# Attention steps in another order: turn of the probabilities, scores, then the product with the values

## The chip, the cores and the metric

One core of a Trainium2 chip runs one program. The time is device microseconds (us) of an execution. The kernel before took 1731.72 us, the median of three runs (1726.76 to 1733.15). Five engines work side by side, each with its own queue of instructions in order: TensorE (PE in the rows; PEld is its loading of weights), VectorE (DVE), ScalarE (ACT), GpSimd (POOL) and SyncE (SP). They meet through semaphores only.

## The reference

Two layers of a hybrid trunk run over 384 tokens (256 latent, 128 context), width 1024, in float32. Each layer has four token mixers on the same normalised input (A: mLSTM; B: neighbourhood attention with a bias table, 8 heads; C: sliding-window attention with a sink, 8 query heads on 2 key heads; D: differential attention, 4 heads of two maps), a gated merge of their outputs, an output projection, and a mixture of experts. The part that the change touches is

```python
s = q @ k.T * scale (+ bias or window, + sink logit)
p = softmax(s)                 # D: p = softmax(s0) - lam * softmax(s1)
out = p @ v
```

Latent queries see the 256 latent keys and 128 cached ones; context queries see the 128 context keys.

## The kernel before

**The list of steps.** The function `schedule()` writes the whole layer out as one list, `SCHEDULE`, and every engine's program walks this list and issues its own part of each step (`for s in SCHEDULE`). So a step's place in the list is its place in the queues of TensorE, VectorE and ScalarE alike. Both layers run the same loop body.

**Gemm units.** The backbone of the list is 102 units `("gemm", g)`. A unit is 128x1024 weights in float32, which ScalarE splits into a high part `whi` (L974) and GpSimd into a low part `wlo` (L810), two units ahead; TensorE takes three products per block (L1340 to L1342), 18 matmuls for three token tiles, into the banks `G`. `("rest", g, t)` is the remainder of a unit from tile t on, so that steps can stand inside a unit. In `branch` units VectorE evicts `G` (L1999), in `proj` and `gate` units ScalarE does.

**Attention.** A unit of attention is a type (B, C, D), a token tile t (0, 1 latent; 2 context, with 128 keys only) and j of 4: 12 units per type, two heads or two maps each. `attention(g, first)` lays their steps out as a pipeline of 15 slots, i = 0 to 14, one after each gemm unit from g on for i < 9, and two per unit after that. A slot holds `sn` of unit i-1, `pv` of i-3, `pt` of i-2 and `sc` of i. What each step issues:

- `sc`: TensorE computes the scores into the banks `S0` and `S1` (L1638, L1639, or L1641 for the context tile). VectorE adds the bias or window (L1860, `prob<-S,bias`, types B and C of latent tiles), takes the maximum (L2144) and its negative (L2151; C has three small instructions). ScalarE takes the exponentials (L1183; C also one of the sink), and issues the load of the next bias, and after the last unit of a type the load of keys.
- `sn`: VectorE takes the reciprocal (L2160) and scales `prob` (L2168; D: L2162 to L2164).
- `pt`: TensorE transposes `prob` into the banks `T0` and `T1` (L1652); ScalarE copies `T0` (L1200) and, in B and C, VectorE copies `T1` (L2175) into `probT`.
- `pv`: TensorE multiplies by the values into the bank `O` (L1682, B and C, 64 output rows at a time; L1679, D). In B and C ScalarE copies `O` rounded to `bhi` (L1212) and VectorE then subtracts it from `O` into `blo` (L1860, `blo<-O,bhi`); in D ScalarE alone copies it (L1206). After the last unit of a type ScalarE issues the load of the next values.

`prob`, `probT` and the softmax's small tiles have two buffers, used in turn by unit; `S`, `T` and `O` have one set. Before TensorE writes a bank, `free(...)` makes it wait for the engine that last read it: `pv` waits for the `blo` (D: the copy) of the unit before, `pt` for the copies of `T0` and `T1`.

**What else shares these queues and banks.** `mod` (L1397): in every fourth such step TensorE multiplies four weight blocks into `O`; it waits until `O` is free. `modv` copies the result on ScalarE (L1134), `modt` turns it in `T1` (L1420). `tp` (L1558) turns `q` and `k` of the next type in the `T` banks, with copies by ScalarE (L1145, L1148). `rope`: VectorE rotates `q` and `k` of D, three tensor_tensor and then two (L1860, `pB<-pA,rope_t` and `pA<-pB`), placed behind the slots that follow gemm 43, 45, 47 and 49 (type B's slots 3, 5, 7 and, two slots later in the list, 10). B's attention starts at gemm 40, C's at 52, D's at 64; `mod` steps stand after the first tile of gemm 55, 59, 67, 71, 76 and others.

The order within a slot comes from the order of the `append` calls in `attention` alone.

Of the kernel before, what the change touches and what calls it, by code (L numbers as in the profile page):

```python
# [108 lines left out]
def schedule():  # L109

    after = {g: [] for g in range(-1, NG)}
    inner = {}

    def put(g, *steps):
        after[g] += steps

    def put_inside(g, t, *steps):

        inner.setdefault((g, t), []).extend(steps)

    put(0, *(("mod", j) for j in range(NEXT, NEXT + MQ)))
    put(1, ("quad3",))
    put(0, ("dma", "stateC"))
    put(4, ("mgate",))
    put_inside(5, 1, ("mturn",))
    put(5, ("tp", "A", "q", 0), ("tp", "A", "q", 1))
    put(6, ("tp", "A", "q", 2), ("tp", "A", "q", 3), ("mcum",))
    put(9, ("tp", "A", "k", 0), ("tp", "A", "k", 1))
    put(10, ("tp", "A", "k", 2), ("tp", "A", "k", 3))
    for m in range(len(MU)):  # L130
        put(9 + 4 * m, ("md", m))
        put(11 + 4 * m, ("m1", m))
        put(13 + 4 * m, ("m2", m))
        put(14 + 4 * m, ("m3", m))
    put(LAST_UNIT[CHUNK_NO["Bv"]] + 2, ("dma", "outB"))
    put(LAST_UNIT[CHUNK_NO["Ckv"]] + 2, ("dma", "outC"))
    put(35, ("dma", "loadB"), ("hn", 0))
    put(37, ("hr", 0))
    for i in range(4):
        put(36 + i, ("tp", "B", "q", i), ("tp", "B", "k", i))  # L140
    put(LAST_UNIT[CHUNK_NO["Dv"]] + 2, ("dma", "outD"))

    def attention(g, first):
        for i in range(12 + 3):
            at = []
            if 1 <= i < 13:
                at.append(("sn", first + i - 1))
            if i >= 3:
                at.append(("pv", first + i - 3))
            if 2 <= i < 14:  # L150
                at.append(("pt", first + i - 2))
            if i < 12:
                at.append(("sc", first + i))
            if i < 9:
                put(g + i, *at)
            elif i % 2:
                put_inside(g + 9 + (i - 9) // 2, 1, *at)
            else:
                put(g + 9 + (i - 9) // 2, *at)
        return g + 12  # L160

    g = attention(40, 0)
    for i in range(4):
        put(40 + i // 2, ("to", 0, i))
    for at, r in zip(ROPE_AFTER, ROPE):
        put(at, ("rope",) + r)
    for i in range(4):
        put_inside(g - 3 + i // 2, 2, ("tp", "C", "q", i))
    put_inside(g - 1, 2, ("tp", "C", "k", 0), ("tp", "C", "k", 1))
    g = attention(g, 12)  # L170
    for i in range(4):
        put_inside(g - 3 + i // 2, 2, ("tp", "D", "q", i))
        put_inside(g - 1 + i // 2, 2, ("tp", "D", "k", i))
    g = attention(g, 24)
    put(g, ("hn", 1))
    put(g + 1, ("hr", 1))
    for i in range(4):
        put(g + 5, ("to", 1, i))
    d_done = g + 5
    for j in range(16, NMOD):  # L180
        q = 36 + j // MQ * MQ + MQ - 1
        q += q in (63, 75)
        put_inside(q, 1, ("mod", j))
        if j % KD == KD - 1:
            put_inside(q, 1, ("modv", j // KD))
            put(37 + j, ("modt", j // KD))
    put(36 + 30, ("gt", 0))
    put(36 + 33, ("gout", 0))
    put(36 + 50, ("gt", 1))
    put(36 + 53, ("gout", 1))  # L190
    put(g - 5, ("dma", "gate1"))
    for c in range(4):
        put(FIRST_UNIT[CHUNK_NO["branch", (3, 1)]], ("mt", c))
    for c in range(4, 8):
        put(FIRST_UNIT[CHUNK_NO["wout", 0]] + 1, ("mt", c))
    put(max(d_done, LAST_UNIT[CHUNK_NO["gate", (3, 0)]]), ("dma", "loadX"))

    steps = [("norm", 0), ("prepare",)]

    for g in range(NG):  # L200
        steps.append(("gemm", g))
        if g == 1:
            steps.append(("dma", "saveX"))
        for t in range(1, TILES):
            if (g, t) in inner:
                steps += inner[g, t] + [("rest", g, t)]
        steps += after[g]
    branch3 = steps.index(("gemm", FIRST_UNIT[CHUNK_NO["branch", (3, 0)]]))
    assert d_done < NG
    late = [s for s in steps[branch3:] if s in [("to", 1, i) for i in range(4)] or s in (("hn", 1), ("hr", 1)) or  # L210
            (s[0] in ("sc", "sn", "pt", "pv") and s[1] >= 24)]
    steps = steps[:branch3] + late + [s for s in steps[branch3:] if s not in late]
    steps += [("norm", 1)] + [("mod", j) for j in OFFRING] + [("route",), ("experts",), ("end",)]
    return steps
# [2226 lines left out]
```

How the kernel before makes its waits and increments, by code:

```python
        @block.sync  # L647
# [13 lines left out]
                def need(s, i):  # L661
                    sp.wait_ge(s.handle, s.value(l, i))
# [3 lines left out]
                def released(p):  # L666
                    if p < 0:
                        sp.wait_ge(*e_lo.in_tile(l, 0, UT, p))
                    elif gs[p] is None:
                        sp.wait_ge(*mod_pe.at(l, ORDER[p][1] - NEXT))
                    else:
                        sp.wait_ge(*lo_done.at(l, gs[p]))
# [2 lines left out]
                    w_in[p % RAW].of(sp.dma_start(raw[:, p % RAW, :], a["units"][bass.ds(l * NU + p, 1), :, :]  # L677
                                                  .rearrange("a p n -> p (a n)")))
                def layer_of(name, n=1):
                    return a[name][bass.ds(l, 1)]
                pc_in.of(sp.dma_start(pcol[:, :], layer_of("pcol").rearrange("a p n -> p (a n)")))
                for p in range(RAW):
                    released(p - RAW)
                    load(p)
                sp.wait_ge(*layer_end.at(l, -1))
                for i in range(MQ):
                    lq_in.of(sp.dma_start(late_home[i], a["units"][bass.ds(l * NU + (RINGN + NEXT + i), 1), :, :]
                                          .rearrange("a p n -> p (a n)")))
# [8 lines left out]
                        p += 1  # L699
                    elif s == ("dma", "saveX"):
                        sp.wait_ge(tokens_in, 16 * TILES)
                        sp.wait_ge(*layer_end.at(l, -1))
# [91 lines left out]
                def need(s, i):  # L794
                    pool.wait_ge(s.handle, s.value(l, i))
```

## Time and profile before

| what | value |
|---|---|
| median of three runs | 1731.72 us (1726.76 to 1733.15) |
| the profiled execution | 1727.18 us, of which the span of the trace is 1725.2 us |
| granted clock of TensorE, mean | 0.997 |
| busy: TensorE, VectorE, ScalarE, GpSimd | 97%, 61%, 51%, 38% |
| type B's attention, layer 0 | about 249 to 329 us from the span's start |
| type C's | about 333 to 413 us |
| type D's | from about 420 us |

A row of a timeline has the start in us from the span's start, the duration in us, the engine, the line, the operation, output<-inputs, the shape (for matmuls rows*columns of the array in use, then the moving operand) and a count; in brackets stands idle time of the engine just before it and what ended it. Instructions of one group that follow each other are merged in one row. Matmuls overlap, so the distance from start to start is what one costs. `whi` rows on ScalarE stand in the gemm step that follows a slot.

### The profile page before, as it was taken

The page shows a single profiled execution, that of the slowest core. Times are in us where ns is not written, and L with a number is a line of the kernel's source. Part 1 is how long each engine was busy: PE and PEld are TensorE (multiplying, and loading weights), DVE is VectorE, ACT ScalarE, POOL GpSimd, SP SyncE. Part 2 cuts the span into 40 slices and gives each one's busy share as a digit, 9 for nine tenths or more (in the row PEclk, how much of TensorE's full clock was granted, in tenths as well). Part 3 has the DMA queues.
Part 4 walks back from the last instruction along what each step waited for, and adds up shares of the span by engine and source line. Part 5 has one row for each costly group of instructions (what it writes and reads, how often), then busy time and mean ns, then how long its engine had stood idle before and what let it go on. Part 6 is the DMA issues. An engine that isn't in the chain of part 4 may idle for free.

```text
span 1725.2 us, 30932 instructions
## 1 busy us (share of the span) xinstructions
PE 1667.7 (97%) x9997; PEld 1329.3 (77%) x9997; DVE 1045.9 (61%) x1868; ACT 872.9 (51%) x1499; POOL 661.8 (38%) x426
## 2 busy tenths in 40 slices
PE   6999999999999999999989999999999999999997
PEld 5788787677888877777767888777778887777775
DVE  3127577564461189999850374775635413899997
ACT  2443344444443357788644334454445334587874
POOL 0645563334467621011125555533344765201102
PEclk9999999999999999999999999999999999999999
DMA  8723343343555559999865234334354553999994
GB/s 335 269 90 103 105 147 125 102 178 136 186 196 217 184 192 408 372 370 366 304 224 196 98 104 138 108 121 146 123 184 160 208 200 142 336 385 370 372 365 157
DMA packets 120847, 367.46 MB, mean 213 GB/s; under 512 B 11964, under 2 KB 34044, under 8 KB 120704
## 3 DMA queue, kind: packets, MB, share of 16 engines
q1 hardware_dynamic: 95024, 323.99, 51.9%
q0 software_dynamic: 6624, 24.18, 3.6%
q10 hardware_dynamic: 19056, 17.52, 3.3%
q8 instruction: 73, 1.20, 0.3%
q14 instruction: 70, 0.57, 0.1%
HBM read 341.71 MB, written 23.93 MB: 212 GB/s over the span
## 4 chain that ended last, share of the span: by engine, by line
PE 52%; issue 17%; DVE 14%; POOL 8%; ACT 4%; DMA 3%; SPq 1%; ACTq 0%; DVEq 0%; POOLq 0%
PE G L1340 13%; PE G L1342 12%; PE G L1341 11%; POOL wlo L810 6%; DVE wlo L1860 4%; ACT whi L982 2%; PE O L1397 2%; PE T L1652 2%; PE S L1638 1%; DMA x_scratch<-pA 1%; DVE pA L1860 1%; PE O L1682 1%; PE S L1340 1%; DVE pB L1860 1%; PE S L1342 1%
## 5 line engine op out<-in xcount | busy, mean ns | idle before, releaser
L810 POOL TENSOR_TENSOR wlo<-raw,whi 128x1024 fp32r<-128x1024 f32 x198 | 483.0, 2445 | 571.3 <-ACT whi L974 571.2
L1340 PE MATMUL G<-whi,hhi 128*128 128x512 f32 (+1 forms) x1440 | 578.5, 402 | 12.3 <-DVE wlo L1860 6.4
L1342 PE MATMUL G<-whi,hlo 128*128 128x512 f32 (+1 forms) x1440 | 557.7, 387 | 0.0
L1341 PE MATMUL G<-wlo,hhi 128*128 128x512 f32 (+1 forms) x1440 | 557.1, 387 | 0.0
L1340 PEld LDWEIGHTS G<-whi,hhi 128*128 128x128 f32 x1440 | 270.4, 188 | 90.7 <-DVE wlo L1860 16.5
L1342 PEld LDWEIGHTS G<-whi,hlo 128*128 128x128 f32 x1440 | 270.5, 188 | 57.5
L1341 PEld LDWEIGHTS G<-wlo,hhi 128*128 128x128 f32 x1440 | 271.1, 188 | 46.9
L974 ACT ACTIVATE whi<-raw 128x1024 fp32r<-128x1024 f32 x204 | 214.6, 1054 | 106.9 <-PE G L1342 71.2
L1860 DVE TENSOR_TENSOR wlo<-raw,whi 128x1024 fp32r<-128x1024 f32 x150 | 179.8, 1220 | 6.3 <-ACT whi L982 3.3
L982 ACT ACTIVATE whi<-raw 128x1024 fp32r<-128x1024 f32 x144 | 152.6, 1060 | 32.5 <-PE G L1342 18.5
L1183 ACT ACTIVATE prob<-prob,am 128x384 f32<-128x384 f32 x64 | 38.9, 609 | 117.0 <-DVE am L2151 58.7
L982 ACT ACTIVATE whi<-pA 128x1024 fp32r<-128x1024 f32 x72 | 76.4, 1062 | 41.7 <-PE G L1342 23.0
L1860 DVE TENSOR_TENSOR wlo<-pA,whi 128x1024 fp32r<-128x1024 f32 x72 | 88.0, 1224 | 15.5 <-ACT whi L982 13.3
L1860 DVE TENSOR_TENSOR wlo<-pB,whi 128x1024 fp32r<-128x1024 f32 x72 | 85.2, 1224 | 6.9 <-ACT whi L982 6.3
L1340 PE MATMUL S<-whi,ehi 128*128 128x512 f32 x192 | 79.4, 414 | 6.4 <-DVE elo L1860 6.3
L982 ACT ACTIVATE whi<-pB 128x1024 fp32r<-128x1024 f32 x72 | 75.1, 1057 | 10.9 <-PE G L1342 10.6
L1340 PE MATMUL G<-whi,bhi 128*128 128x512 f32 x192 | 79.2, 412 | 0.0
L1342 PE MATMUL S<-whi,elo 128*128 128x512 f32 x192 | 75.4, 393 | 0.0
L1341 PE MATMUL S<-wlo,ehi 128*128 128x512 f32 x192 | 75.2, 391 | 0.0
L1342 PE MATMUL G<-whi,blo 128*128 128x512 f32 x192 | 75.1, 391 | 0.0
L1341 PE MATMUL G<-wlo,bhi 128*128 128x512 f32 x192 | 74.9, 390 | 0.0
L805 POOL TENSOR_TENSOR sink_col<-ones 128x1 f32<-128x1 f32 x26 | 15.5, 597 | 149.7 <-ACT yo L1276 76.8
(384 smaller groups left out, 2411.0 us busy)
## 6 DMA issues: line engine op xcount, KB each, us to landing
raw<-in_units SPq DMA_DIRECT2D x426, 512.0 KB, 5.1
pA<-in_units SPq DMA_DIRECT2D x78, 512.0 KB, 5.9
pB<-in_units SPq DMA_DIRECT2D x72, 512.0 KB, 6.3
h_sorted<-sig POOLq DMA_DIRECT2D x12, 514.0 KB, 7.1
hs<-h_sorted POOLq DMA_DIRECT2D x10, 514.0 KB, 7.4
y_sorted<-yo POOLq DMA_DIRECT2D x10, 512.0 KB, 7.1
bias<-in_nat_bias ACTq DMA_DIRECT2D x16, 256.0 KB, 3.2
kT<-in_units SPq DMA_DIRECT2D x6, 512.0 KB, 4.8
```

What stands on the lines that cost most here:

```text
L810: lo_done.of(nc.gpsimd.tensor_tensor(wlo[:, k, :], raw[:, POS_OF[g] % RAW, :], whi[:, k, :].bitcast(F32), ALU.subtract))
L974: hi_done.of(nc.scalar.activation(whi[:, g % CONV, :], raw[:, p % RAW, :], ACT.Copy))
L982: hi_done.of(nc.scalar.activation(whi[:, n % CONV, :], expert_raw(n), ACT.Copy))
L1183: e = nc.scalar.activation(prob[:, u % 2, m, 0:w], src, ACT.Exp, bias=am[:, u % 2, m:m + 1], accum_out=am[:, u % 2, 2 + m:3 + m])
L1340: nc.tensor.matmul(dst, st_hi, mv_hi, start=start, stop=False)
L1341: nc.tensor.matmul(dst, st_hi, mv_lo, start=False, stop=False)
L1342: return nc.tensor.matmul(dst, st_lo, mv_hi, start=False, stop=stop)
L1397: mm = nc.tensor.matmul(O[32 * q:32 * q + 32, c0:c0 + P], cond[:, k, :], raw[:, MODPOS[j - MQ + 1 + q] % RAW, k * P:(k + 1) * P], start=(k ...
L1638: nc.tensor.matmul(S[:, m, 0:256], q, kT[r, kj, 0:256], start=True, stop=True)
L1652: mm = nc.tensor.transpose(T[:, m, b * P:(b + 1) * P], prob[:, u % 2, m, b * P:(b + 1) * P], ident[:, :])
L1682: mm = nc.tensor.matmul(O[64 * m:64 * m + 64, 0:P], values(b, lo, 64), pr, **fl)
L1860: return V.tensor_tensor(o, i0, i1, op)
```

## The change

In `attention`, the `append` of `pv` moves behind those of `pt` and `sc`. A slot is then `sn` of unit i-1, `pt` of i-2, `sc` of i, `pv` of i-3, on every engine that has a part in them. Slots with two of the steps (12, 13) turn `pv`, `pt` into `pt`, `pv`; slots 0 to 2 and 14 are as before. Each step's instructions, waits and buffers are unchanged.

```diff
@@ -145,12 +145,12 @@
             at = []
             if 1 <= i < 13:
                 at.append(("sn", first + i - 1))
-            if i >= 3:
-                at.append(("pv", first + i - 3))
             if 2 <= i < 14:
                 at.append(("pt", first + i - 2))
             if i < 12:
                 at.append(("sc", first + i))
+            if i >= 3:
+                at.append(("pv", first + i - 3))
             if i < 9:
                 put(g + i, *at)
             elif i % 2:
```

## Rows read from the trace of the kernel before

**Rows 1.** The profile page, busy time (share of the span) and instructions of each engine.

```profile
PE 1667.7 (97%) x9997; PEld 1329.3 (77%) x9997; DVE 1045.9 (61%) x1868; ACT 872.9 (51%) x1499; POOL 661.8 (38%) x426
```

**Rows 2.** Timeline of TensorE, slot 3 of type B, and slot 5's start (start us, duration us, engine, line, what, count).

```profile
267.54 0.39 PE L1342 MATMUL G<-whi,hlo 128*128 128x512 f32 x1
...
267.86 0.66 PE L1682 MATMUL O<-probT,pB 128*64 128x128 f32 x8
...
268.66 0.88 PE L1652 MATMUL T<-ident,prob 128*128 128x128 f32 x6
...
269.47 0.71 PE L1638 MATMUL S<-kT,qT 64*128 64x256 f32 x4
...
270.33 0.50 PE L1340 MATMUL G<-whi,hhi 128*128 128x512 f32 x1
...
281.42 0.66 PE L1682 MATMUL O<-probT,pB 128*64 128x128 f32 x8
```

**Rows 3.** Timeline of TensorE: slot 2 of type C; slot 14 of type B.

```profile
343.42 0.39 PE L1342 MATMUL G<-whi,hlo 128*128 128x512 f32 x1
...
343.66 0.81 PE L1652 MATMUL T<-ident,prob 128*128 128x128 f32 x6
...
344.40 0.71 PE L1638 MATMUL S<-kT,qT 64*128 64x256 f32 x4
...
328.69 0.44 PE L1682 MATMUL O<-probT,pB 128*64 128x128 f32 x4
...
329.06 0.50 PE L1340 MATMUL G<-whi,hhi 128*128 128x512 f32 x1
```

**Rows 4.** Timelines of VectorE, ScalarE and GpSimd, type B, slots 3 to 7.

```profile
270.80 0.96 DVE L1860 TENSOR_TENSOR prob<-S,bias 128x768 f32<-128x768 f32 x1 [0.24 <-DMA bias<-in_nat_bias]
...
273.06 1.36 DVE L1860 TENSOR_TENSOR pB<-pA,rope_t 128x512 f32<-128x512 f32 x3
...
275.33 2.90 DVE L2168 TENSOR_SCALAR prob<-prob,am 128x384 f32<-128x384 f32 x2
...
278.15 0.28 DVE L1860 TENSOR_TENSOR blo<-O,bhi 128x128 fp32r<-128x128 f32 x1
...
278.35 0.54 DVE L2175 COPY probT<-T 128x384 f32<-128x384 f32 x1
...
278.81 0.94 DVE L1860 TENSOR_TENSOR prob<-S,bias 128x768 f32<-128x768 f32 x1
...
297.16 0.75 DVE L2168 TENSOR_SCALAR prob<-prob,am 128x384 f32<-128x384 f32 x2
...
274.20 1.04 ACT L974 ACTIVATE whi<-raw 128x1024 fp32r<-128x1024 f32 x1
...
289.89 0.26 ACT L1212 ACTIVATE bhi<-O 128x128 fp32r<-128x128 f32 x1
...
275.32 2.36 POOL L810 TENSOR_TENSOR wlo<-raw,whi 128x1024 fp32r<-128x1024 f32 x1 [3.24 <-ACT whi L974]
```

**Rows 5.** Timelines of VectorE and GpSimd, a rope step of the mLSTM stretch.

```profile
147.89 2.40 DVE L1860 TENSOR_TENSOR pB<-pC,rope_t 128x512 f32<-128x512 f32 x1
...
147.34 5.21 POOL L810 TENSOR_TENSOR wlo<-raw,whi 128x1024 fp32r<-128x1024 f32 x2 [6.02 <-ACT whi L974]
```

**Rows 6.** Timeline of TensorE, two waits in attention: slot 9 of B, slot 12 of C.

```profile
307.21 0.66 PE L1682 MATMUL O<-probT,pB 128*64 128x128 f32 x8 [1.76 <-DVE probT L2175]
...
406.92 0.44 PE L1652 MATMUL T<-ident,prob 128*128 128x128 f32 x2 [0.99 <-ACT qT L1145]
```

**Rows 7.** Timelines of TensorE and ScalarE around `mod`, in type C and in type D.

```profile
376.13 1.95 PE L1397 MATMUL O<-raw,cond 128*32 128x128 f32 x64
...
379.53 1.04 ACT L974 ACTIVATE whi<-raw 128x1024 fp32r<-128x1024 f32 x1
...
460.46 1.96 PE L1397 MATMUL O<-raw,cond 128*32 128x128 f32 x64
...
461.41 1.05 ACT L974 ACTIVATE whi<-raw 128x1024 fp32r<-128x1024 f32 x1
```

## The prediction

> **What bounds the kernel now.** I read first the busy times: TensorE is busy for 97% of the span [rows 1], so whatever lengthens or shortens TensorE's own queue in the attention stretch appears in the time one for one, and whatever happens on other engines counts only where TensorE waits for it. Then TensorE's timeline through one attention slot: between two gemm units come the product with the values (`pv`), the turn of the probabilities (`pt`), and the scores (`sc`) [rows 2]. Then VectorE, ScalarE and GpSimd through the same slots, because the list of steps is walked by every engine: the diff moves the eviction of `O` behind the softmax of the newer unit on ScalarE and VectorE too. I write E for the moment when ScalarE has finished a slot's exponentials and starts its next instruction. In the before kernel VectorE spends the time up to E on other work, the rope step above all: its row starts 1.14 us before E, while the exponentials run [rows 4]. The second layer's attention rows repeat the first's, so all that follows is worked out for layer 0 and doubled.
>
> **What is removed: one switch of the array's shape per slot, on the path.** For the unit types B and C, `pv` is 128*64, `sc` is 64*128, and gemm and `pt` are 128*128. From the last gemm matmul to the next one, a full slot takes 0.32 + 0.80 + 0.81 + 0.86 = 2.79 us [rows 2]. With `pt` first, gemm to `pt` is 0.24 and `pt` to `sc` 0.74, seen in a slot that has no `pv` [rows 3]. `pv` to gemm costs what `pv` to `pt` does: 0.37 for four matmuls [rows 3], 0.80 for twelve [rows 2]. Only `sc` to `pv` is shown nowhere. A switch shows as 0.08 us ahead of it (0.32 against 0.24) and 0.07 behind it (0.81 against 0.74), 0.15 in all. From below `sc` to `pv` costs no switch (0.15 less than `sc` to gemm), from above two (0.15 more); I take 0.86 as for `sc` to gemm, the nearest row, since it too is one switch. The new slot is 0.24 + 0.74 + 0.86 + 0.80 = 2.64, a gain of 0.15 us (0 to 0.3). Nine slots of B and nine of C per layer have all three steps: 18 x 0.15 = -2.7 us per layer. Type D's `pv` is 128*128, and keeps its number of switches: 0. The Trainium skill, page TensorEngine Tiling (Array Packing), section Key Properties, says that changing the tiling mode drains TensorE. That speaks for the change; by the whole 0.39 us of a gemm matmul per drain it would be -7 us per layer instead; rows 2 and 3 show less than half of that.
>
> **What is added: the eviction of `O` stands behind the exponentials.** The copy `bhi` (0.26 us) now runs at E, and VectorE's `blo` waits for it, at E + 0.3. Behind `blo` in VectorE's queue stand the rope step, the branch evictions, the next normalisation (`sn`), the copy of `T1`, and the next scores' bias add. Who waits: the next `pv` and the `mod` matmuls (both want `O`), and `pt` (wants `sn` and `T1`).
> A plain slot: `blo` at E + 0.3, reciprocal E + 0.5, scaling E + 0.7 (0.75 us [rows 4]), copy of `T1` E + 1.4, bias add E + 1.85. From bias add to its own E it is 274.20 - 270.80 = 3.4 us [rows 4], so the next E is at E + 5.25.
> A slot with rope (four of B's): rope starts at E + 0.5 instead of before E. GpSimd's `wlo` subtraction began 1.12 us after E and lasted 2.36 [rows 4]; with the copy ahead of `whi` it runs from about E + 1.3 to E + 3.7. VectorE is held by such an instruction: the 2.90 us of two scalings that take 0.75 elsewhere [rows 4], and one rope instruction of 2.40 us where three take 1.36 [rows 5]. Two of the rope instructions (0.45 each) get through before it, the rest (2.27 - 0.9 = 1.4 up to the scaling) follows: scaling at E + 5.1, copy at E + 5.8, bias add at E + 6.25, next E at E + 9.65.
> The Trainium skill, page SBUF — State Buffer, section Who interferes with whom, gives this as a rule: two-input VectorE instructions and GpSimd exclude each other. By this rule, the trace agrees, and the rope cannot slip through.
> VectorE's pair of slots becomes 14.9 us. TensorE's is 281.42 - 267.86 = 13.56 us [rows 2], less 0.3 for two switches. VectorE, hidden until now, is 1.6 us too slow per pair.
> - Slot 5: `pv` wants `O` at 281.42 - 0.38 + 1.60 = 282.64; it is free at 274.20 + 9.65 + 0.6 = 284.45: +1.8 us.
> - Slot 7: the same excess again, +1.6 us.
> - Slot 9: `pt` waits for the copy of `T1` and `sc` for the exponentials, together 3.5 us, less the 1.76 us that stand there now [rows 6]: +1.7 us.
> - Slots 10 and 12: `pt` now has nothing in front of it while the copies of the turned `q` and `k` leave the `T` banks; the turn between them waits for a later `T1` copy: +0.45, +0.6, +0.5. The same wait in type C is 0.99 us now, behind `pv` [rows 6]; there it costs +0.65 and +0.3.
> Sum of B: 6.7 - 1.3 = +5.4 us per layer.
> **C.** No rope, so VectorE keeps up (5.5 us against 6.6), with the branch evictions too. But after slot 6 four `mod` matmul groups want `O` at 376.13 - 0.6 = 375.5, and slot 6's E is 379.53 [rows 7], 1.15 us earlier in the new order because `sc` no longer stands behind `pv` and three slots are shorter. `O` is free at E + 0.6 = 379.0: +3.5 us. The next turn of `mod` values no longer waits 0.2 us. C: 3.5 + 0.95 - 0.2 - 1.35 = +2.9 us.
> **D.** VectorE has no part in its `pv`. The `mod` matmuls at 460.46 want `O`, whose copy ends 0.28 us after E, 461.41 - 0.67 [rows 7], so at 461.0: +0.6 us. The scores' 0.67 us earlier start is otherwise covered by gemms.
> Queues: no DMA moves past another; the bias loads keep their place in the `sc` step, the loads of keys and values theirs, SP's and GpSimd's lists are unchanged. The split into `whi` comes 0.16 us later per slot and up to 2 us later behind a late E; its result is wanted a whole gemm unit (some 4 us) later, so it costs nothing; without that cover it would be those 2 us again.
>
> **Sum.** 5.4 + 2.9 + 0.6 = 8.9 us per layer, +17.9 us in all. Against the profiled execution (1727.2 us) this gives 1745.1; the median of the runs shown lies 4.5 us higher, so 1749.6 by it, and one of its three runs is as low as the profiled one. I forecast 1748.
>
> **Rivals.**
> *Rope escapes the hold* (it starts early enough, or GpSimd later). Then only the scaling is held, until E + 3.7 as now; VectorE's pair is 13.5 us, B costs about +0.9 instead of +5.4: 4.4 x 2 = +9 us, 1740. For it: the margin at the third rope instruction is 0.1 us. Against it: the instructions behind the third would be caught instead [rows 5].
> *C's scaling is caught as well.* In C one small instruction more stands ahead of it, so its second half starts about E + 1.25, GpSimd at E + 1.3. If GpSimd wins, each C slot's `sn` is 2.3 us later, VectorE needs 8.4 us per slot against 6.6, and the wait at `mod` grows by about 4 us per layer: 1757.
> *The other side: the saved switches decide.* If `O` is never late (the copy at E + 0.3 is reached before `pv` asks, because the earlier `sc` pulls E forward by more than rope pushes it back), only -2.7 us per layer is left: 1726, within 0.5%. It decides once E + 0.6 lies before `pv`'s turn, 1.6 us after the slot begins; in plain slots this holds with over 1 us in hand, in the slots after rope it misses by 1.8. The drain rule of the Trainium skill named above, at its full 0.39 us per switch, would make this one 1717.
> *The order of the other engines doesn't matter* (the change acts as its words say, on TensorE alone): then -5 us from switches and the three stalls kept, the same 1726. The code speaks against it, since all engines walk one list.
>
> **How the numbers follow.** Forecast 0.48; rope escapes 0.14; C caught too 0.16; saved switches, by either way, 0.22. About 0.5% (8.6 us) is what a measurement of this kernel can tell from no change. Slower by more than that: 0.48 + 0.16 + half of the rope case (1740 lies on the bound) = 0.71. The 0.22 splits into 0.06 faster, if a switch costs more than I take, and 0.16 the same, with the other half of the rope case 0.23. The range goes from 1728, between the switch case and the rope case, to 1760, past the C case. The forecast's own range is 1742 to 1754.
>
> **What would show it.** Right: in the waits of TensorE, new rows in which `O` (the lines of `pv` and of `mod`) waits for `blo` by VectorE, 1.5 us each in slots 5 and 7 and 3.5 us at C's `mod`; rope rows on VectorE of 3 us or more beside a `wlo` row of GpSimd; full slots of 2.64 us instead of 2.79. Wrong: rope still at 1.36 us, no wait at `mod`, or full slots as long as before. If no wait on `O` is over 1 us, my account of VectorE's queue fails as a whole; if the waits are there and the slots of B lag by less than 1 us each, only the hold by GpSimd does.

## The result, and the profile after

The changed kernel takes 1765.21 us (median of four runs, 1761.8 to 1766.3) beside 1729.24 for the kernel before on the same chip: 1.0206 times as long, 95% interval 1.019 to 1.0221. I had forecast 1748, with a range from 1728 to 1760. The sign was right, and the size was half of what came: +17.9 us forecast, +36 measured.

The page's busy times of the changed kernel:

```profile
PE 1681.4 (95%) x9997; PEld 1343.4 (76%) x9997; DVE 1047.0 (59%) x1868; ACT 869.8 (49%) x1499; POOL 659.8 (37%) x426
```

TensorE has the same 9997 matmuls as in [rows 1], but is busy for 13.7 us more. The switches that were saved should not have made this more. So besides new waits, some matmuls ran slower. The span of the trace rose by 39.4 us, of which 25.7 are idle time of TensorE.

The waits of TensorE, whole span (the bank it wanted, its line, who let go of it: us in total, times, longest):

```profile
PE O L1682 <- DVE blo L1860: 9.5, 6, 1.7
PE O L1397 <- issue: 6.9, 2, 3.5
...
PE T L1652 <- DVE probT L2175: 5.5, 2, 2.8
...
PE O L1397 <- ACT pA L1206: 3.8, 2, 1.9
PE T L1558 <- DVE probT L2175: 3.6, 2, 1.8
PE T L1652 <- ACT qT L1145: 2.6, 4, 0.9
PE T L1652 <- DVE modc L1860: 2.3, 2, 1.2
```

The forecast's new waits are all here: `pv` (L1682) on `blo`, and `mod` (L1397) on the bank `O`. Two more are not in my sum: the last row, and a third wait per layer in the first row (I had two, slots 5 and 7). Every count is a multiple of two, one for each layer.

TensorE's timeline, type B, layer 0: slot 3 whole, then the rows with a wait in slots 5, 7 and 9 and in the turn of C's `q`:

```profile
270.03 0.39 PE L1342 MATMUL G<-whi,hlo 128*128 128x512 f32 x1
270.26 0.82 PE L1652 MATMUL T<-ident,prob 128*128 128x128 f32 x6
271.00 0.71 PE L1638 MATMUL S<-kT,qT 64*128 64x256 f32 x4
...
271.87 0.66 PE L1682 MATMUL O<-probT,pB 128*64 128x128 f32 x8
...
272.67 0.50 PE L1340 MATMUL G<-whi,hhi 128*128 128x512 f32 x1
...
286.77 0.66 PE L1682 MATMUL O<-probT,pB 128*64 128x128 f32 x8 [1.56 <-DVE blo L1860]
...
301.78 0.66 PE L1682 MATMUL O<-probT,pB 128*64 128x128 f32 x8 [1.66 <-DVE blo L1860]
...
313.26 0.88 PE L1652 MATMUL T<-ident,prob 128*128 128x128 f32 x6 [2.79 <-DVE probT L2175]
314.64 0.49 PE L1641 MATMUL S<-kT,qT 64*128 64x128 f32 x4 [0.50 <-ACT prob L1183]
315.13 1.12 PE L1682 MATMUL O<-probT,pB 128*64 128x128 f32 x8
...
328.87 0.55 PE L1558 MATMUL T<-ident,pC 128*128 128x128 f32 x3 [1.76 <-DVE probT L2175]
```

The slot is 272.67 - 270.03 = 2.64 us, as worked out, against 2.79 in [rows 2]. The waits in slots 5, 7 and 9 (1.56, 1.66 and 2.79 + 0.50) are near the prediction's 1.8, 1.6 and 3.5. The row at 315.13 is the surprise: eight matmuls that take 0.66 us everywhere else take 1.12.

TensorE's timeline again: C's and D's `mod` matmuls, and in C the `pv` of slot 6 and the turn of slot 9:

```profile
384.04 0.66 PE L1682 MATMUL O<-probT,pC 128*64 128x128 f32 x8 [1.67 <-DVE blo L1860]
...
389.97 3.55 PE L1397 MATMUL O<-raw,cond 128*32 128x128 f32 x64 [3.47 <-issue]
...
407.94 0.84 PE L1652 MATMUL T<-ident,prob 128*128 128x128 f32 x6 [1.15 <-DVE modc L1860]
...
478.63 3.48 PE L1397 MATMUL O<-raw,cond 128*32 128x128 f32 x64 [1.88 <-ACT pA L1206]
```

The same stretches in the table of windows (busy time of each engine, then the granted clock):

```profile
core 0: us, PE busy (x) PEld busy (x) DVE busy (x) ACT busy (x) POOL busy (x), PEclk, DMA share, GB/s
...
315.00:318.40 3.40, 3.40 (x20) 2.64 (x17) 2.25 (x11) 2.32 (x8) 0.00 (x0) 0.50 0.02 5
390.00:393.50 3.50, 3.50 (x65) 3.12 (x65) 0.88 (x3) 0.49 (x1) 2.56 (x1) 0.52 0.02 5
478.80:482.30 3.50, 3.50 (x65) 3.12 (x58) 1.01 (x3) 0.73 (x1) 2.45 (x1) 0.51 0.02 5
```

Three times per layer TensorE comes back from a long wait and is granted the lower of its two levels, 1.2 GHz instead of 2.4, for some 3.4 us. `mod` then takes 3.55 and 3.48 us instead of the 1.95 and 1.96 of [rows 7]. The trace of before shows no such fall in attention, not even behind its wait of 1.76 us [rows 6].

Laid side by side, the two traces part by 35.4 us in attention: 6.7 in B, 7.0 in C and 4.3 in D in layer 0, and 17.5 in all in layer 1. The other 4 us lie at the first gemm units (2.3, from 31 to 54 us) and between the layers (1.6). The change touches nothing there. The clock does: the changed kernel's trace has a granted clock of 0.72 from 30 to 36 us and of 0.59 from 892 to 896, and the trace of before has 1.00 at both places. Such falls come and go there in the traces of the other kernels below too, so I don't count these 4 us to the change.

### The profile page after: what moved, and what is told of

Read it like the earlier page. It is cut to its first block, busy times and chain, and to the rows that moved or that the text cites. A ratio compares the mean times of both kernels' runs of the same rounds, so it can differ in the third digit from the quotient of the medians.

```text
span 1764.6 us, 30952 instructions
## 1 busy us (share of the span) xinstructions
PE 1681.4 (95%) x9997; PEld 1343.4 (76%) x9997; DVE 1047.0 (59%) x1868; ACT 869.8 (49%) x1499; POOL 659.8 (37%) x426
## 3 DMA queue, kind: packets, MB, share of 16 engines
q8 instruction: 75, 1.23, 0.3%
## 4 chain that ended last, share of the span: by engine, by line
PE 52%; DVE 18%; issue 14%; POOL 5%; ACT 5%; DMA 4%; SPq 1%; ACTq 1%; DVEq 0%; POOLq 0%
PE G L1340 13%; PE G L1342 12%; PE G L1341 12%; DVE wlo L1860 4%; POOL wlo L810 4%; ACT whi L982 2%; PE O L1397 2%; DVE pB L1860 2%; DVE am L2144 2%; DMA x_scratch<-pA 1%; DVE pA L1860 1%; PE S L1340 1%; DVE prob L1860 1%; DMA bias<-in_nat_bias 1%; ACT prob L1183 1%
## 5 line engine op out<-in xcount | busy, mean ns | idle before, releaser
L1183 ACT ACTIVATE prob<-S,am 128x128 f32<-128x128 f32 (+1 forms) x80 | 35.5, 449 | 81.4 <-DVE am L2151 67.7
```

The source lines that it names most:

```text
L1183: e = nc.scalar.activation(prob[:, u % 2, m, 0:w], src, ACT.Exp, bias=am[:, u % 2, m:m + 1], accum_out=am[:, u % 2, 2 + m:3 + m])
```

## The experiments

In all of them `schedule` takes a function that gives `pv`'s place in a slot: 0 first as before, 1 behind `pt`, 2 last as in the changed kernel. TensorE, ScalarE and VectorE may each walk a list of their own:

```diff
-            if i >= 3:
-                at.append(("pv", first + i - 3))
+            pv = [("pv", first + i - 3)] if i >= 3 else []
+            place = where(first, i)
+            if place == 0:
+                at += pv
             if 2 <= i < 14:
                 at.append(("pt", first + i - 2))
+            if place == 1:
+                at += pv
             if i < 12:
                 at.append(("sc", first + i))
+            if place == 2:
+                at += pv
...
-                for s in SCHEDULE:
+                for s in WALK["pe"]:
```

The diffs below show only these places. Line numbers in these kernels are 10 higher (`rope ahead` 14; with dummies 11 to 17). Every ratio is against the kernel before on the same chip.

**Which engine's order costs?** First TensorE's order alone:

```diff
+PE_WHERE = lambda first, i: 2
+ACT_WHERE = lambda first, i: 0
+DVE_WHERE = lambda first, i: 0
```

> TensorE walks the new order (turn, scores, values); ScalarE and VectorE keep the old one (eviction of O first). Theory 1 (the loss comes from the eviction's place on ScalarE and VectorE, not from TensorE's order): the waits for O at slots 5 and 7 of type B and at the mod steps are gone, no half-clock window in attention, full slots stay 0.15 us shorter; 1729 - 5 + 2 for the turns that wait for the T banks = 1726 (1720 to 1732). Rival (TensorE's own order costs it): at least 1755.

Measured: 1745.11 us, 1.0088 (1.0072 to 1.0105). Both missed. No wait on `O` over 0.3 us is left, but VectorE now stands at `blo` for a `pv` that comes late, ahead of its copy of `T1` (in slot 3 for 0.96 us, 0.16 in the kernel before). TensorE's wait for that copy rose to 3.1 us in slot 9, and the clock fell behind it. In C four waits of 0.95 to 1.60 us on the `T` banks and the scores cost about 3 us more per layer. Then the other two engines' order alone:

```diff
+PE_WHERE = lambda first, i: 0
+ACT_WHERE = lambda first, i: 2
+DVE_WHERE = lambda first, i: 2
```

> The opposite split: TensorE keeps the old order, ScalarE and VectorE take the new one (eviction of O behind the exponentials). Theory 1: as slow as the changed kernel or slower, since O is free as late and TensorE asks for it 1.6 us earlier in a slot: 1770 (1760 to 1785), with the waits for O on the line of the values in slots 5 and 7. Rival (TensorE's order costs it): 1729.

Measured: 1779.39 us, 1.028 (1.0263 to 1.0297), as the theory said, and the worst of all. Its waits of TensorE:

```profile
PE O L1692 <- DVE blo L1870: 29.9, 21, 3.7
...
PE O L1407 <- issue: 6.2, 2, 3.1
```

`pv` asks for `O` at the head of the slot and gets it behind the exponentials. So most of the loss comes from the place of the eviction, and a late `pv` on TensorE softens it; but TensorE's new order alone isn't free either.

**The eviction ahead of the exponentials, TensorE still in the new order.**

```diff
+PE_WHERE = lambda first, i: 2
+ACT_WHERE = lambda first, i: 1
+DVE_WHERE = lambda first, i: 2
```

> TensorE in the new order; ScalarE copies O ahead of the exponentials (turn, values, scores); VectorE subtracts behind the new maximum (turn, scores, values), while the exponentials run. Theory 1: what hurts is the copy behind the exponentials, which makes VectorE wait for them; here VectorE's part is covered, rope stays at 1.4 us, no wait for O over 0.5 us: 1725 (1719 to 1731). Rival (anything of the eviction behind the scores on VectorE costs): over 1740.

Measured: 1733.88 us, 1.0023 (1.0014 to 1.0033). Of the 36 us all but 4 are gone. The only difference from the changed kernel is the place of one 0.26 us copy per unit on ScalarE. The miss of 9 us against my 1725 has one place; TensorE's timeline at C's `mod`:

```profile
379.60 3.46 PE L1407 MATMUL O<-raw,cond 128*32 128x128 f32 x64 [2.44 <-issue]
```

`blo` still stands behind VectorE's part of the scores, so `mod` waits 2.44 us and then runs at the low clock: some 4 us per layer. The next run takes that away and nothing else:

```diff
-PE_WHERE = lambda first, i: 2
-ACT_WHERE = lambda first, i: 1
-DVE_WHERE = lambda first, i: 2
+PE_WHERE = lambda first, i: 0 if (first, i) == (12, 6) else 2
+ACT_WHERE = lambda first, i: 0 if (first, i) == (12, 6) else 1
+DVE_WHERE = lambda first, i: 0 if (first, i) == (12, 6) else 2
```

> As e3_copy_first (TensorE in the new order, ScalarE copies O ahead of the exponentials, VectorE's subtraction last), but the one slot of C ahead of the mod matmuls keeps pv first on all engines. Theory (the shape switches saved are worth 0.15 us in 18 slots per layer, and e3 gave them back in the mod wait of 2.6 us and a low-clock stretch behind it): no mod wait, no low-clock stretch in attention, 1733.9 - 2 x (2.5 + 1.6) = 1725.7 us (1722 to 1729), below the kernel before by 4 us. Rival (switches save nothing in the end, because TensorE's other waits grow by as much): 1729 or more.

Measured: 1726.67 us, 0.9976 (0.9965 to 0.9986): below the kernel before, by about the 4 us that the theory gave. It is the one version here that beats both kernels. TensorE's timeline in that slot:

```profile
373.34 0.66 PE L1692 MATMUL O<-probT,pC 128*64 128x128 f32 x8 [0.96 <-DVE blo L1870]
...
377.41 1.95 PE L1407 MATMUL O<-raw,cond 128*32 128x128 f32 x64
```

`pv`, now first in its slot, pays 0.96 us (0.59 in layer 1), and `mod` pays nothing. The switches' gain is real, but smaller than the medians make it look. 17 slots of 0.15 us are 2.6 us per layer. Laid beside the trace of before, this one gains 0.14 us in each slot without a new wait, some 2.1 us per layer, and gives back the 0.96 or 0.59 us at `pv` and 0.4 to 0.5 us at the end of B, where a `T` bank is waited for. Attention as a whole is shorter by 0.5 us in layer 0 and 1.1 in layer 1, so by 1.6 us. The ratio says 4 us (2.4 to 6.1). The falls of the clock outside attention, which are there in some executions and not in others, are a likely part of the rest, and that isn't shown.

VectorE's eviction moved ahead of its scores as well was no better:

```diff
+PE_WHERE = lambda first, i: 2
+ACT_WHERE = lambda first, i: 1
+DVE_WHERE = lambda first, i: 1
```

> TensorE in the new order (pt, scores, pv), ScalarE and VectorE in the order pt, pv, scores: the eviction of O stands ahead of the softmax of the newer unit, but behind the copies of T0 and T1. Theory (the loss comes from the eviction standing behind the exponentials, the gain from the saved switches of the array's shape is real): no wait on O by pv or mod over 0.5 us, no low-clock stretch in attention, slots of 2.64 us: 1726 us (1720 to 1731). Rival (the scores' bias add now waits for the late pv, so the softmax starts 0.8 us later and the waits move to pt in the slots after rope): 1735 or more.

Measured: 1740.47 us, 1.0059 (1.0038 to 1.0081), the rival. No wait on `O` over 0.3 us is left, but the bias add now stands behind a subtraction that waits for the late `pv`; in slot 9 the turn waits 2.50 us and the scores 0.70, and the clock falls once per layer. An engine that works in order should not have an instruction that must still wait placed ahead of work that it could already do.

**Is it the rope?** The changed kernel, with VectorE's rotation ahead of `pv`'s part:

```diff
         put(at, ("rope",) + r)
+        if r[0] == "D":
+            a = after[at]
+            k = next(n for n, s in enumerate(a) if s[0] == "pv")
+            a.insert(k, a.pop())
```

> The changed kernel with the four rope steps of type B one place earlier on VectorE, ahead of the eviction of O, so that they run under the exponentials again. Theory 1: rope rows back at 1.36 us, the waits at slots 5 and 7 gone and the one at slot 9 back near 1.8; B's part of the loss (6.7 us a layer) falls to about 1, C's and D's (11.3 us a layer) stay: 1765 - 11 = 1754 (1749 to 1759). Rival (rope under GpSimd's hold isn't what loses B's time): within 3 us of 1765.

Measured: 1745.52 us, 1.0095 (1.0078 to 1.0112): 20 us less than the changed kernel, where 11 were expected. The waits say where (again us in total, times, longest):

```profile
PE O L1411 <- issue: 6.9, 2, 3.5
...
PE T L1666 <- DVE probT L2189: 2.1, 2, 1.1
PE O L1696 <- DVE blo L1874: 2.0, 2, 1.1
```

The waits of B's slots 5 and 7 are gone, and slot 9's is 1.1 us instead of 2.8; those of `mod` stand untouched. B, which lost 6.6 us per layer in the changed kernel's trace, now gains 0.6. The rest of the miss is the clock. It no longer falls in B, which fits the shorter wait, but it also falls behind only one of the four `mod` waits. VectorE and GpSimd in a rope slot of the changed kernel:

```profile
307.34 0.29 DVE L1860 TENSOR_TENSOR blo<-O,bhi 128x128 fp32r<-128x128 f32 x1 [1.53 <-ACT bhi L1212]
307.55 3.54 DVE L1860 TENSOR_TENSOR pB<-pA,rope_t 128x512 f32<-128x512 f32 x3
...
308.33 2.48 POOL L810 TENSOR_TENSOR wlo<-raw,whi 128x1024 fp32r<-128x1024 f32 x1 [3.49 <-ACT whi L974]
```

The three rope instructions take 3.54 us instead of the 1.36 of [rows 4], because the third is held by `wlo`. The Trainium skill, page SBUF — State Buffer, section Who interferes with whom, calls the port pair that the two engines share an exclusive lock. The row agrees: the excess, 2.18 us, is most of `wlo`'s 2.48. In the run with the rope ahead all four rotations of B take 1.36 us again. That run takes away the hold and the rope's place behind the exponentials together, so it doesn't say how much of B's loss is due to each.

**What does the clock cost?** The changed kernel with dummy matmuls of the identity where TensorE waits anyway, so that it is busy but no other step moves:

```diff
                         if j % MQ == 0:
+                            if j in FILL:
+                                free("T0")
+                                keep_busy(T[:, 0, 0:P], FILL[j])
                             free("O")
...
                     elif s[0] == "pt":
...
+                        if u == 7:
+                            free("T0")
+                            keep_busy(T[:, 0, 0:P], 22)
                         need(pn_dve, u)
...
+FILL = {20: 28, 32: 14}
```

> The changed kernel, with dummy matmuls of the identity issued where TensorE waits longest: 28 ahead of C's mod group, 14 ahead of D's, 22 ahead of the turn in slot 9 of B (into T0 once its copy has been read). Nothing else moves. They are meant to fit inside the waits of 3.5, 1.9 and 2.8 us. Theory (part of the excess over my forecast is the clock, which falls to half for 3.41 us behind a wait): the six low-clock stretches of attention go, the mod rows are 1.95 us again, and with up to 1.6 us saved at each the time is 1757 us (1753 to 1761). Rival (the clock's fall costs nothing, because TensorE is limited by the other engines there): 1765, unchanged, or more where the dummies overrun.

Measured: 1767.58 us, 1.0222 (1.0201 to 1.0244): nothing decided by the time alone, since the dummies were twice as long as I took them to be. TensorE's timeline in C:

```profile
384.51 6.41 PE L1389 MATMUL T<-ident 128*128 128x128 f32 x56
390.85 1.96 PE L1411 MATMUL O<-raw,cond 128*32 128x128 f32 x64
```

28 dummies are 56 records and take 6.41 us, 2.9 more than the wait; with B's 1.8 and D's 1.4 that is 12 us too much in the two layers, and yet the time rose by only 2.4 (1.0222 against 1.0206). The counts halved (`FILL = {20: 14, 32: 7}`, and 11):

> As e6_fill, with half as many dummy matmuls, since one took 0.23 us there and they overran the waits by 1.8, 2.9 and 1.4 us per layer: 14 ahead of C's mod group (3.2 us into a wait of 3.5), 7 ahead of D's (1.6 into 1.9), 11 ahead of slot 9's turn in B (2.5 into 2.8). Theory (the clock's fall behind the waits costs up to 1.6 us each, six times): mod rows of 1.95 us, no low-clock stretch in attention, 1756 us (1753 to 1759). Rival (e6_fill's 1767.6 with 12 us of overrun is explained in some other way, the clock costs nothing): 1765.

Measured: 1755.67 us, 1.0148 (1.0131 to 1.0165), as the theory said. Timeline of TensorE in C:

```profile
383.83 1.28 PE L1389 MATMUL T<-ident 128*128 128x128 f32 x10
385.42 1.96 PE L1411 MATMUL O<-raw,cond 128*32 128x128 f32 x64 [0.30 <-DVE blo L1877]
```

`mod` gets `O` as late as before (5.9 us behind the `pv` of slot 6 in both traces), takes 1.96 us, and the granted clock is 1.00 through attention. The falls are worth the difference of the two ratios, 1.0206 - 1.0148, which is 10 us with an interval of some 6 to 14 (the medians differ by 9.5). Laid side by side, the two traces say the same: against the kernel before, attention is longer by 25.4 us here and by 35.4 in the changed kernel, again 10.0. Of these, 1.5 us aren't the clock: `pv` in slot 6 of C waits 0.87 and 0.70 us here instead of 1.67 and 1.36, for a load that came earlier (told with the window's load below). The rest, 8.5 us, is 1.0 us per fall in B, where a wait of 0.40 us on a `T` bank shows again that the low clock had hidden, and 1.6 in C and D. Six stretches of 3.4 us at half clock can cost 6 x 1.7 = 10 us at most.

**Do the types' losses add up?** One type at a time in the new order on all engines:

```diff
+WHERE = lambda first, i: 2 if first == 0 else 0    # B; C: first == 12; D: first == 24
```

> The new order in type B alone, the old one in C and D, on all engines. Theory (the losses of the three types are separate and add up; the trace of the changed kernel lost 6.7 us per layer in B, one low-clock stretch of slot 9 among it): 2 x 6.7 above the kernel before, 1743 us (1739 to 1747). Rival (B's lag is made up by C, or C's waits at mod are B's lag carried over): 1735 or less, or 1755 or more with mod waits in C still there.

> The new order in type C alone, the old one in B and D, on all engines. Theory (the types' losses are separate; the trace of the changed kernel lost 7.0 us per layer in C: the mod wait 3.5, the low clock behind it 1.6, pv held in slot 6 1.7, turn in slot 9 1.15, end of the type 0.9, less 1.35 for switches): 2 x 7.0, 1743.5 us (1740 to 1747), with those four waits in the trace at C's places. Rival (part of C's waits is B's lag, carried over): 1737 or less.

> The new order in type D alone, the old one in B and C, on all engines. Theory (D loses 4.3 us per layer in the changed kernel's trace: the mod wait of 1.9 and the low clock behind it 1.6 above all): 1738 us (1735 to 1741) if the clock falls behind a wait of only 1.9 us here too; about 1734 if it does not. Rival (D's lag comes from C's): below 1732.

Measured: B 1744.21 us, 1.0084 (1.0062 to 1.0106); C 1743.16 us, 1.008 (1.0062 to 1.0097); D 1736.78 us, 1.0036 (1.0024 to 1.0049). All three lie in the ranges given. D's range was given for a fall of the clock behind its `mod`, which the trace shows in both layers; but of its eight executions two took 1740 us and six 1734.5 to 1737, so the fall is probably not there each time. 0.0084 + 0.0080 + 0.0036 = 0.0200 beside 0.0206 for the whole change: the losses are separate. From C's run and D's, the waits of TensorE:

```profile
PE O L1407 <- issue: 6.9, 2, 3.5
...
PE O L1692 <- DVE blo L1870: 3.3, 2, 1.8
...
PE T L1662 <- DVE modc L1870: 2.3, 2, 1.1
```

```profile
PE O L1407 <- ACT pA L1216: 3.8, 2, 1.9
```

C's waits on `blo` and on `modc` are there with B untouched, so they are C's own, not B's lag carried over.

**Undoing the change only ahead of `mod`.**

```diff
+WHERE = lambda first, i: 0 if (first, i) in ((12, 6), (24, 6)) else 2
```

> The changed kernel, but in the one slot of C and the one of D that stand ahead of a group of mod matmuls, pv keeps its old place on all three engines. Theory (the mod matmuls find O held by the eviction behind the exponentials, and TensorE's granted clock falls to half behind these waits): the mod waits of 3.5 us (C) and 1.9 us (D) and the two low-clock stretches (mod rows of 3.5 us instead of 1.95) go, while C's pv of that slot, now 1.6 us earlier in the queue, waits about 1.6 us more for blo: -(3.5 + 1.6 - 1.6 + 1.9 + 1.6) = -7 us per layer, 1751 us (1746 to 1756). Rival (the lag is VectorE's as a whole and only shows elsewhere when the mod wait is taken away): 1760 or more, with the waits moved to the pv and pt of the following slots.

Measured: 1755.36 us, 1.014 (1.0113 to 1.0166), inside the range, 4 us above its middle. TensorE's timeline in C:

```profile
384.46 1.12 PE L1692 MATMUL O<-probT,pC 128*64 128x128 f32 x8 [2.87 <-DVE blo L1870]
```

`mod` waits no longer, in C or D. But in C the wait (2.87 us, 3.40 in layer 1) and the low clock moved to `pv`, 5 us ahead of it: while the eviction of every slot stands behind the exponentials, the first user of `O` that comes early pays. In D, where `pv` waits for only 0.38 us, the gain was kept.

## Why the prediction was off by half

**Right: the switches** (-2.7 us per layer). The slot is 2.64 us, 0.15 less than before, and the trace of the version with late `pv` and early eviction shows 0.14 in each slot without a new wait, some 2.1 us per layer. The Trainium skill, page TensorEngine Tiling (Array Packing), section Key Properties, says that such a change drains TensorE. The runs agree that it costs, but less than half of the 0.39 us of a gemm matmul that the prediction tried.

**Right: B** (+5.4 per layer, without the clock). Waits of 1.56, 1.66 and 3.29 us for a forecast of 1.8, 1.6 and 3.5, the turn's 1.76 (1.23 before, so +0.5 for a forecast of +0.6) and slot 12's 0.45 for 0.5. B alone cost 14.3 us by the medians. In its trace B is longer by 6.3 us in layer 0, where the clock fell behind slot 9, and by 5.4 in layer 1, where it didn't. The rival in which the rope escapes is refuted by the row of 3.54 us. The rival in which saved switches decide is refuted as well, and the one by which the order of the other engines doesn't matter by the first two runs: their order alone costs 50 us.

**Right: C's wait at `mod`**, 3.47 us for 3.5, and the T-bank wait in slot 12.

**Wrong: "`O` is free at E + 0.6 = 379.0: +3.5 us", with nothing after it.** This is the step that failed most: my sum priced each wait by its length and let the matmuls behind it run at their old durations. In the changed kernel each wait of 1.88 to 3.5 us is also followed by some 3.4 us at 1.2 GHz, 1.0 to 1.6 us more each time. No term of the sum and no rival had it. The six falls are 8.5 us: nearly half of what was missed. With the dummies in, the kernel is at 1755.7, inside my range, though still above the 1754 at which the forecast's own range ends.

**Wrong: "No rope, so VectorE keeps up (5.5 us against 6.6), with the branch evictions too."** VectorE and GpSimd in C, from the scores of slot 4 to the eviction of slot 6 (the first row is from the kernel before, slot 4):

```profile
361.26 0.96 DVE L1860 TENSOR_TENSOR prob<-S,bias 128x768 f32<-128x768 f32 x1 [0.48 <-PE S L1639]
...
370.61 0.96 DVE L1860 TENSOR_TENSOR prob<-S,bias 128x768 f32<-128x768 f32 x1 [1.78 <-DMA bias<-in_swa_mask]
...
374.78 0.29 DVE L1860 TENSOR_TENSOR blo<-O,bhi 128x128 fp32r<-128x128 f32 x1 [1.63 <-ACT bhi L1212]
375.13 1.88 DVE L1999 SCALAR_TENSOR_TENSOR pB<-sig,G 128x512 f32<-128x512 f32 x3
376.93 1.24 DVE L1860 TENSOR_TENSOR am<-am 128x2 f32<-128x2 f32 x1
...
383.69 0.29 DVE L1860 TENSOR_TENSOR blo<-O,bhi 128x128 fp32r<-128x128 f32 x1 [1.63 <-ACT bhi L1212]
...
389.57 0.29 DVE L1860 TENSOR_TENSOR blo<-O,bhi 128x128 fp32r<-128x128 f32 x1 [1.63 <-ACT bhi L1212]
...
375.77 2.39 POOL L810 TENSOR_TENSOR wlo<-raw,whi 128x1024 fp32r<-128x1024 f32 x1 [5.47 <-ACT whi L974]
```

A plain unit of C takes VectorE 389.57 - 383.69 = 5.9 us, but the one before it takes 8.9, against TensorE's 6.6. Two things were missing from my 5.5. The three branch evictions (1.88 us) used to begin under the exponentials (at 363.99 us, 1.15 before E) and now stand behind `blo`. And they push the addition of two numbers per partition into `wlo`'s time, so that it takes 1.24 us instead of the 0.15 of other slots. This is the rival "C's scaling is caught as well", but in one slot and not in all. Its price of 1757 lies nearer to the result than my forecast, for another reason.

A third thing came on top, and it is what "the bias loads keep their place" left out: the scores of slot 4 wait 1.78 us (1.47 in layer 1) for the load of C's window. ScalarE issues that load with the exponentials of the unit before. It landed 3.2 us after its issue in the kernel before, and 4.0 to 4.9 us after it here; why it took longer isn't shown. Slot 6's `pv` then waits 1.67 us (1.36). The two go together: in the five traces with C's eviction behind the exponentials and slot 6 in the new order, ten layers in all, `pv`'s wait runs from 0.70 to 1.92 us and the load's from 0.81 to 2.01, and `pv`'s is each time 0.09 to 0.12 us the shorter. So with the load in time this wait would nearly vanish, and without the hold it would be 1.1 us shorter. No run took either away.

Slot 9's wait of 1.15 us on `modc` is one that I did not look for: that copy follows `blo` in VectorE's queue too. Together 2.8 us per layer.

**Mis-sized: "so at 461.0: +0.6 us"** in D. It was 1.88: in the new order the negation of the maximum falls into `wlo`'s time (1.36 us instead of 0.26), and E is later by about as much (VectorE, D's slot 6):

```profile
475.79 1.36 DVE L2151 TENSOR_SCALAR am<-am 128x2 f32<-128x2 f32 x1
```

Set against the stretches of the trace of layer 0, with the clock taken off (1.0, 1.6 and 1.6 us): B 5.6 us (forecast 5.4), C 5.4 (2.9), D 2.7 (0.6; besides `mod`, a later `pv` of D waits 0.38 us, which I did not have either). For two layers 17.9 forecast + 8.5 (clock) + 2 x 0.2 (B) + 2 x 2.5 (C) + 2 x 2.1 (D) = 36.0 us, beside 35.4 in the traces' attention and 36.0 between the medians. The clock's part is shown by the run with the dummies; the runs with C and D alone show that their losses are their own. That GpSimd holds the two small instructions, and that C's load comes late, is read from the traces.

## What to carry to other kernels

When a step moves in a list that all engines walk, move it on each engine apart: TensorE wants the product late (fewer switches), but its eviction belongs ahead of the long softmax and behind the copies that others wait for, and ahead of a second user of the bank the old order may be the better one. Price a new wait of some 2 us or more on TensorE at its length, and let the range reach some 1.6 us beyond it for the clock; where it can't be avoided, matmuls of the identity inside it gave that back here. In an engine's queue look also at the shortest instructions: 1.24 us under a hold is eight times their 0.15. And ask of each load whether the time between its issue and its use has shrunk.

## What the runs showed of the hardware

The fall of the clock isn't decided by the length of the last wait alone. The same wait of 1.88 us at D's `mod` was followed by low clock in the changed kernel and by full clock in layer 0 of the kernel with the rope ahead:

```profile
469.17 1.95 PE L1411 MATMUL O<-raw,cond 128*32 128x128 f32 x64 [1.88 <-ACT pA L1220]
...
382.00:386.00 4.00, 3.86 (x73) 3.35 (x74) 1.02 (x5) 1.05 (x2) 2.60 (x1) 1.00 0.17 41
```

The row of 382 to 386 us lies behind a wait of 3.46 us at C's `mod`, also at full clock. There are more such cases: with the eviction alone moved, `mod` in C waited 3.08 us in both layers and ran at full clock, and with B alone in the new order slot 9's wait of 2.7 us was followed by low clock in layer 0 and by full clock in layer 1. So an edit that shifts a wait in time can lose or win some 1.6 us that has nothing to do with its own work. Why it fell in one case and not in the other stays open.

The kernel before has a spread of its own, and it goes with the clock. Of its 42 executions beside these experiments, the five with a mean granted clock of 0.998 took 1726.4 us on average, the seven with 0.995 took 1730.2, and the three with 0.992 took 1733.5. A difference of a few us between two kernels is better read from the same stretch of both traces, with its granted clock, than from two medians.
